# Rope columns of the second block's input projection as f32 column groups of the raw residual

## The chip, the core and the metric

The kernel runs on one core of a Trainium2 chip. The time is the device time of one execution in microseconds (us). Three runs of the kernel before gave 1178.18, 1178.46 and 1178.75 us; the median, 1178.46 us, is what the changed kernel is compared with. A core has five engines that run side by side and meet only at semaphores: PE (TensorE, the matrix engine), DVE (VectorE), ACT (ScalarE), POOL (GpSimd) and SP (SyncE, which here only issues transfers). Each engine takes its own instructions strictly in order.

## What is computed

Two transformer blocks over 512 tokens of 1024 features, all in f32. The change touches the start of the second block: a norm with a gain, a scale and a shift (the modulation), then one projection whose columns are the latent queries (256), the latent keys and values (128), the 32 rope columns of the keys, and the queries, keys and values of the chunked attention.

```python
h = modulate(rmsnorm_2(x, g_attn_norm[l]), sh_a, sc_a)      # h = norm * (1 + sc) + sh, per feature
proj = jnp.dot(h, w_in[l])
q_lat, kv_lat, k_rope, ca_qkv = jnp.split(proj, split_pts, axis=-1)   # 256, 128, 32, 1536 columns
...
k = jnp.concatenate([k_nope, broadcast(k_rope)], axis=-1)   # the same 32 columns for all 8 heads
k = rmsnorm_2(k, g_mla_k[l])
k = jnp.concatenate([k[..., :64], rope(k[..., 64:], positions)], axis=-1)
```

The input x of this block is itself a norm of the first block's result. Both norms divide by the root of a mean of squares over the features of one token, so together they are one factor per feature (`modA`) and one factor per token, called the root below; the shift `mod[:, 0, :]` is added behind both.

## The kernel before

**Layout and products.** Activations lie with the features on the 128 partitions and the 512 tokens along them, so a tile is 128x512. The residual is `h`, eight tiles (KD = 8). A product in f32 precision is made of three cheaper ones (`split_product`, L1550 is its matmul): each operand is split in a high and a low part of a reduced f32 type (`xh`, `xl` for activations, `wh`, `wl` for weights), and high·high, high·low and low·high are summed in PSUM. An output tile of 128 columns of the projection over 1024 features is so 8 x 3 = 24 matmuls. A matmul whose operands stay plain f32 needs no split; the trace shows it as two records.

**Weights.** They come in chunks of 128x2048, two slots each of `raw`, `wh` and `wl`. SP issues the transfer of chunk n once chunk n-2 has been split. ACT makes `wh` (`split_next`, `split_quarter`: L625, L643), once the products that read the slot before are done. POOL then makes `wl` = `raw` - `wh` (`low`, `low_edge`: L478, L506). PE waits for `lo_done`. So between "slot free" and "chunk usable" lie one ACT pass, one POOL pass and whatever stands ahead of them in these two queues.

**The place of the change.** In the second block's stream (`STREAM2`) the first chunk is "kvr": the latent keys and values (tile e=0) and the rope columns (tile e=1: the 32 columns twice and their halves swapped twice, 128 in all). The second, "ql", holds the two tiles of the latent queries, and four chunks "cqk" follow. `normed_pair` computes the two tiles of the first chunk in two halves of 256 tokens, while DVE (`norm_tiles`, L1104 and L1112) and ACT (`norm_high`, L683) still make `xh` and `xl` tile by tile: PE waits for each `norm.lo`. The root of a half stands in bank 2 or 3 (`SS_BANKS`, `rstd(j)`), the norm's tiles pass through banks 4, 5 and 7. Then PE computes the two ql tiles into banks 2 and 3, then the first cqk chunk into banks 6 and 7.

**ACT's order there** is written out by hand: the last `norm_high` tiles; `load_rel` (four transfers of the bias table, issued from ACT's own queue, L912 and L913); the logarithm and exponential of the final norm's sum (L662, L664); `split_next(base, ...)`, which is `wh` of the first cqk chunk (L625); the squares of the finished tiles (L931, L950). POOL's `wl` of that chunk (L478) comes behind the L625. DVE squares are split with L1430, the rope tile is turned by its cosines with L1436 to L1443.

**The same form elsewhere.** The first block has a projection of 8 columns padded to 32 that is done in plain f32 from the raw `h`: eight products 32 columns wide, each into its own quarter of the output partitions (L1826); a later product with a 0/1 matrix (`quarter_ones`, L1833) adds the four quarters. The changed kernel uses this form for the rope columns.

Of the kernel before, what the change touches and what calls it, by code (L numbers as in the profile page):

```python
# [7 lines left out]
ALU = mybir.AluOpType  # L8
# [41 lines left out]
STREAM2 = [("kvr", 1), ("ql", 1), ("cqk", PAIRS), ("cv", 2), ("mq", 1), ("mkv", 1), ("out", KD // 2), ("up", KF)]  # L50
# [37 lines left out]
def build(nc, x_first, xT, cols_in, stream1, down1, stream2, down2, ada, c_row, w_spatial_T, b_spatial_rows, w_gate, quarter_sum, positions, rel_tiles, outT):  # L88
    ctx = ExitStack()
    with ctx:  # L90
# [28 lines left out]
        sb("to_row", [P, ROW_PAD])  # L119
# [169 lines left out]
        rope.dve, rope.sq = sems("rope", "dve", "sq")  # L289
# [13 lines left out]
        P2 = {"kv": 1, "rope": 2, "ql": [3, 4], "q": [5, 7, 9, 11], "k": [6, 8, 10, 12], "v_first": 13, "v": [14, 15, 16, 17]}  # L303
# [68 lines left out]
        CSIL_HALVES = [ss_final, bank[7]]  # L372
        gate_raw, gate_weights = [lf[b][:, 0:KD * GATE_COLS] for b in range(2)]
# [101 lines left out]
        def _(pool):  # L475
# [83 lines left out]
            lows(N1, base - 1, DOWN_CHUNK)  # L559
            slot = (base - 1) % 2  # L560
# [58 lines left out]
        def _(act):  # L619
# [286 lines left out]
            act.dma_start(pos_i, positions.partition_broadcast(P)).then_inc(pos_landed, 16)  # L906
            residual_down(res_down1, norm_final, BASE1["down"], (cosines, sines))
# [7 lines left out]
            norm_rsqrt(norm_attn2, 0, eps2_c)  # L915

            def last_half():
# [3 lines left out]
                      | quarters(N1 + N_DOWN - 1, res_down1.mm, 2 * KD + 1, (9, 10, 11, 12)))  # L921
            act.wait_ge(res_down1.h, KD + 1)
# [21 lines left out]
            split_next(base, p2.mm, P2["rope"])  # L944
# [5 lines left out]
            act.activation(sqk[0][0:96, :], bank[1][0:96, :], ACT.Square).then_inc(rope.sq, 1)  # L950
            lat_square_high(0, sq2[0])
            head_square(sq2[1][:, :], bank[2][:, :], P2["ql"][0])
            act.wait_ge(norm_attn2.lo, 2 * KD)
            head_square(scratch[3][:, :], bank[3][:, :], P2["ql"][1])
            lat_square_high(1, sq2[1])
            lat_square_high(2, scratch[3])
            split_next(base + 1, p2.mm, P2["ql"][1])
            act.wait_ge(rope.sq, 1)
            act.activation(rope_sq[0:96, :], sqk[0][0:96, :], ACT.Copy).then_inc(rope.sq, 1)
# [111 lines left out]
        def _(dve):  # L1071
# [325 lines left out]
            def angles():  # L1397

                dve.wait_ge(pos_landed, 16)
# [52 lines left out]
            for t in range(2):  # L1452
                dve.scalar_tensor_tensor(scratch[2 + t][:, :], bank[2 + t][:, :], col("ql_g", t), r[:, :], ALU.mult, ALU.mult).then_inc(head.pre, 1)
# [93 lines left out]
        def _(pe):  # L1547
# [20 lines left out]
            def normed_pair(banks, slot, mm, norm, aside, at=3, quarter0=None):  # L1568


                for j in range(2):
                    for k in range(KD):
                        if j == 0 and k == at:
                            aside()
                        if quarter0 is not None and j == 0 and k in (0, 2, 4):
# [113 lines left out]
            def residual_down(L, res, base, norm):  # L1689
# [26 lines left out]
                for m, j, e in ((KD - 2, None, 0), (KD - 2, None, 1), (KD - 1, 0, 0), (KD - 1, 0, 1), (KD - 1, 1, 0), (KD - 1, 1, 1)):  # L1716
# [8 lines left out]
                    for kk in range(KF // 2):  # L1725
# [95 lines left out]
            pe.wait_ge(setup1, 10)  # L1821
            pe.wait_ge(p1.act, 1)
            for x in range(KD // QUARTERS):
                for quarter in range(QUARTERS):
                    k, c = QUARTERS * x + quarter, GATE_COLS * quarter
                    ins = pe.matmul(bank[4][c:c + GATE_COLS, :], gate_weights[:, GATE_COLS * k:GATE_COLS * k + GATE_COLS], h[:, k, :],  # L1826
                                    start=x == 0, stop=x == KD // QUARTERS - 1)
            ins.then_inc(p1.mm, 1)
# [85 lines left out]
            def last_sums():  # L1914
                norm_sum(norm_attn2, 1, weighted_acc, KD + 2)
# [3 lines left out]
            normed_pair(bank[0:2], base % 2, p2.mm, norm_attn2, last_sums, 5, KD + 6)  # L1919
            pe.wait_ge(lo_done, base + 2)  # L1920
            for e in range(2):
                features_tile(bank[2 + e], (base + 1) % 2, e).then_inc(p2.mm, 1)
            pe.wait_ge(setup2, 10)

            def pair_sums(p):
                for which in range(2):
                    if p == 0:
                        pe.wait_ge(lat.lo, 3)
# [293 lines left out]
```

## Time and profile before

| | us |
|---|---|
| median of 3 runs | 1178.46 |
| the profiled execution, its own time | 1179.01 |
| span of the profiled execution | 1177.3 |
| PE busy | 1167.2 (99%) |
| PE weight loads | 958.3 (81%) |
| DVE busy | 566.3 (48%) |
| ACT busy | 515.5 (44%) |
| POOL busy | 455.8 (39%) |

The span starts with the first recorded instruction; 1.7 us of the execution's own time lie around it. PE is busy almost all the time and its matmuls overlap in the records (a record of 0.39 us starts every 0.23 us), so for PE the distance between two starts is what a matmul costs, not its duration. Times of day in the text are microseconds from the start of the span of this execution. The granted clock of PE is 1.00 throughout.

### The profile page before, as it was taken

Reading aid. Unit: us, or ns where it says so; the run is one execution under the profiler, and the core shown is the slowest. Engines: PE = TensorE matmul, PEld = TensorE weight load, DVE = VectorE, ACT = ScalarE, POOL = GpSimd, SP = SyncE. Lnnn points to the kernel's source line nnn. Section 1 sums busy time; section 2 is a strip of 40 time slices with the busy share of each in tenths; the row PEclk is TensorE's granted clock in tenths of the full one; section 3 lists DMA queues with packets and bytes.
Section 4 is the critical chain, followed back from the end, with each engine's and each line's share of the span. In section 5 each row is a group of like instructions: output and inputs, shape, how many; then the busy total and the mean of one; then the engine's idle time right before and its main releaser. Section 6 shows DMA issues by size and latency. Waiting matters only on the chain.

```text
span 1177.3 us, 16124 instructions
## 1 busy us (share of the span) xinstructions
PE 1167.2 (99%) x5962; PEld 958.3 (81%) x5962; DVE 566.3 (48%) x1128; ACT 515.5 (44%) x815; POOL 455.8 (39%) x181
## 2 busy tenths in 40 slices
PE   9999999999999999999999999999999999999998
PEld 7787778988888888888988667789888888888887
DVE  4364245977777774212574567726434334440000
ACT  5534653634443432322646576835543443431110
POOL 6541314444434433444443211034434433434442
PEclk9999999999999999999999999999999999999999
DMA  8322122554554542223332110122232223212222
GB/s 302 115 82 98 36 103 78 215 188 174 209 204 171 196 156 94 92 95 110 141 134 77 55 37 1 37 72 74 106 108 102 76 107 107 79 66 99 99 98 96
DMA packets 27714, 132.06 MB, mean 112 GB/s; under 512 B 3472, under 2 KB 4880, under 8 KB 18832
## 3 DMA queue, kind: packets, MB, share of 16 engines
q1 hardware_dynamic: 25776, 128.90, 30.6%
q10 hardware_dynamic: 1888, 2.49, 0.7%
q8 instruction: 32, 0.52, 0.2%
q14 instruction: 18, 0.15, 0.0%
HBM read 129.28 MB, written 2.10 MB: 112 GB/s over the span
## 4 chain that ended last, share of the span: by engine, by line
PE 97%; ACT 2%; issue 0%; POOL 0%; DMA 0%; DVE 0%; DVEq 0%; ACTq 0%
PE psum L1550 86%; PE psum L1619 2%; PE psum L1631 2%; PE psum L2070 1%; PE psum L1780 1%; ACT prob L712 1%; PE psum L1883 1%; PE psum L2006 1%; ACT probT L695 1%; PE psum L1984 0%; POOL wl L494 0%; DMA gains_and_h<-x_first 0%; PE psum L1848 0%; PE psum L2014 0%; PE psum L1589 0%
## 5 line engine op out<-in xcount | busy, mean ns | idle before, releaser
L478 POOL TENSOR_TENSOR wl<-raw,wh 128x2048 fp32r<-128x2048 f32 (+1 forms) x88 | 364.6, 4143 | 497.5 <-ACT wh L628 285.0
L1550 PE MATMUL psum<-xh,wh 128*128 128x512 f32 (+1 forms) x1008 | 382.9, 380 | 1.2 <-POOL wl L494 1.1
L1550 PE MATMUL psum<-xl,wh 128*128 128x512 f32 (+1 forms) x1008 | 378.7, 376 | 0.0
L1550 PE MATMUL psum<-xh,wl 128*128 128x512 f32 (+1 forms) x1008 | 378.6, 376 | 0.0
L1196 DVE SCALAR_TENSOR_TENSOR scratch<-psum,cols,scratch 128x511 f32<-128x511 f32 (+1 forms) x176 | 131.6, 748 | 196.4 <-ACT scratch L773 188.4
L1550 PEld LDWEIGHTS psum<-xh,wh 128*128 128x128 f32 x1008 | 189.5, 188 | 40.1 <-issue 3.1
L1550 PEld LDWEIGHTS psum<-xh,wl 128*128 128x128 f32 x1008 | 189.6, 188 | 34.9
L1550 PEld LDWEIGHTS psum<-xl,wh 128*128 128x128 f32 x1008 | 189.7, 188 | 33.9 <-issue 0.2
L628 ACT ACTIVATE wh<-raw 128x2048 fp32r<-128x2048 f32 (+1 forms) x50 | 88.4, 1768 | 243.8 <-PE psum L1550 243.8
L1550 PE MATMUL psum<-acth,wh 128*128 128x512 f32 (+1 forms) x374 | 141.0, 377 | 0.0
L1550 PE MATMUL psum<-actl,wh 128*128 128x512 f32 (+1 forms) x374 | 140.8, 377 | 0.0
L1550 PE MATMUL psum<-acth,wl 128*128 128x512 f32 (+1 forms) x374 | 140.8, 377 | 0.0
L625 ACT ACTIVATE wh<-raw 128x2048 fp32r<-128x2048 f32 (+1 forms) x41 | 69.3, 1690 | 129.6 <-PE psum L1550 120.8
L1550 PEld LDWEIGHTS psum<-actl,wh 128*128 128x128 f32 x374 | 70.4, 188 | 13.0
L1550 PEld LDWEIGHTS psum<-acth,wh 128*128 128x128 f32 x374 | 70.4, 188 | 12.9
L1550 PEld LDWEIGHTS psum<-acth,wl 128*128 128x128 f32 x374 | 70.4, 188 | 12.8
L494 POOL TENSOR_TENSOR wl<-raw,wh 128x512 fp32r<-128x512 f32 (+1 forms) x28 | 35.5, 1298 | 112.7 <-ACT wh L643 99.8
L773 ACT ACTIVATE scratch<-psum,cols 128x512 f32<-128x512 f32 x88 | 67.6, 768 | 15.5 <-PE psum L1550 13.5
L1119 DVE SCALAR_TENSOR_TENSOR gains_and_h<-psum,mod,gains_and_h 128x512 f32 (+2 forms) x18 | 12.4, 690 | 125.1 <-PE psum L1550 125.1
L1080 DVE CUSTOM_DVE_ANT_0 ada_raw<-ada_raw,ss_final 128x512 f32<-128x512 f32 x42 | 55.2, 1315 | 0.0
L1117 DVE TENSOR_TENSOR gains_and_h<-gains_and_h,psum 128x512 f32<-128x512 f32 (+2 forms) x19 | 11.4, 599 | 80.0 <-PE psum L1550 80.0
L695 ACT ACTIVATE probT<-psum 128x256 f32<-128x256 f32 (+3 forms) x48 | 33.5, 697 | 34.1 <-PE psum L1619 34.1
(269 smaller groups left out, 1384.2 us busy)
## 6 DMA issues: line engine op xcount, KB each, us to landing
raw<-stream SPq DMA_DIRECT2D x69, 1024.0 KB, 4.8
ada_raw<-ada SPq DMA_DIRECT2D x48, 512.0 KB, 5.1
raw<-down SPq DMA_DIRECT2D x32, 704.0 KB, 4.0
outT<-gains_and_h SPq DMA_DIRECT2D x8, 256.0 KB, 5.0
gains_and_h<-xT SPq DMA_DIRECT2D x7, 256.0 KB, 6.4
raw<-stream SPq DMA_DIRECT2D x7, 256.0 KB, 6.8
rel<-rel_tiles ACTq DMA_DIRECT2D x1, 1344.0 KB, 8.7
wsT<-w_spatial_T SPq DMA_DIRECT2D x1, 512.0 KB, 6.1
```

What stands on the lines that cost most here:

```text
L478: pool.tensor_tensor(wl[slot][:, 0:w], raw[slot][:, 0:w], wh[slot][:, 0:w].bitcast(F32), ALU.subtract).then_inc(lo_done, 1)
L494: ins = pool.tensor_tensor(wl[slot][:, part], raw[slot][:, part], wh[slot][:, part].bitcast(F32), ALU.subtract)
L625: act.activation(wh[slot][:, 0:w], raw[slot][:, 0:w], ACT.Copy).then_inc(hi_done, 1)
L628: act.activation(wh[slot][:, 0:w], raw[slot][:, 0:w], ACT.Copy).then_inc(hi_done, 1)
L695: act.activation(probT[V % len(probT)][:, :, 0:w], TURN_BANKS[:, :, 0:w], ACT.Copy).then_inc(att.ptc, 1)
L773: act.activation(scratch[r][:, :], bank[r][:, :], ACT.Identity, bias=col(L.b, i * 4 + r), scale=col(L.w, i * 12 + (3 * r + 2))).then_inc(L ...
L1080: dve.tensor_tensor_reduce(part, part, c, 1.0, 0.0, ALU.mult, ALU.add, mod_sum[:, e, a:a + 1]).then_inc(ada_red, 1)
L1119: dve.scalar_tensor_tensor(h[:, m, tokens], b[:, tokens], mod[:, gain, bass.ds(m, 1)], h[:, m, tokens], ALU.mult, ALU.add).then_inc(res.h, 1)
L1196: dve.scalar_tensor_tensor(scratch[r][:, d:T], bank[r][:, 0:T - d], col(L.w, i * 12 + (3 * r + tap)), scratch[r][:, d:T], ALU.mult, ALU.ad ...
L1550: ins = pe.matmul(out, lhs[a], rhs[b], start=first and n == 0, stop=last and n == 2)
L1619: ins = pe.transpose(TURN_BANKS[:, e, P * j:P * j + P], prob[V % 4][:, e, P * j:P * j + P], ident[:, :])
L1631: ins = pe.matmul(HEADS_BANKS[p % 2][r:r + HD, P * i:P * i + P], v[:, j, c:c + HD], probT[V % len(probT)][:, e, P * j:P * j + P], start=j ...
```

## The change

The rope tile leaves the stream. Chunk one is now "kvq" (latent keys and values, and the first tile of the latent queries) and goes through `normed_pair`; chunk two holds the second query tile alone, half as wide (1024 columns). The rope columns are computed in plain f32 from the raw residual: POOL multiplies the 32 columns per feature tile by `modA`; PE makes eight products into four quarters of bank 4 (`rope_products`), inside the second half of `normed_pair`; ACT copies the quarters to SBUF; DVE multiplies them by the root; ACT adds the shift's share to them; PE adds up and spreads the quarters to the 128 rows with one f32 product with a 0/1 matrix (`rope_turned`), in the middle of the second query tile. The shift's share is eight one-column products of the unscaled columns with `mod[:, 0, k]`, put into the last residual tile of the first block, and copied by ACT behind the first root. The weights and the 0/1 matrix come with one more transfer from ACT's queue.

```diff
-STREAM2 = [("kvr", 1), ("ql", 1), ("cqk", PAIRS), ...
+STREAM2 = [("kvq", 1), ("ql", 1), ("cqk", PAIRS), ...
-    if n == BASE2["mkv"]:
+    if n in (BASE2["ql"], BASE2["mkv"]):
         return CHUNK // 2
...
+        rope_raw, rope_turned = scratch[0][:, 0:ROPE_COLS], scratch[0][:, ROPE_COLS:ROPE_COLS + P]
+        rope_weights = scratch[1][:, 0:ROPE_COLS]
+        rope_parts = bank[4]
+        rope_tile = bank[2]
+        SHIFTS = bank[3][:, 0:1]
+        ql_tiles = [bank[1], bank[3]]
...
             lows(N1, base - 1, DOWN_CHUNK)
+            pool.wait_ge(pos_landed, 32)
+            pool.wait_ge(mod_done, 7)
+            pool.tensor_tensor(rope_weights..., rope_raw..., modA[:, 0, :]..., ALU.mult).then_inc(mod_done, 1)
...
             act.dma_start(pos_i, positions.partition_broadcast(P)).then_inc(pos_landed, 16)
+            act.dma_start(scratch[0][:, 0:ROPE_COLS + P], w_rope[:, :]).then_inc(pos_landed, 16)
...
             norm_rsqrt(norm_attn2, 0, eps2_c)
+            act.wait_ge(p2.mm, P2["shift"])
+            act.activation(rope_shift[:, :], SHIFTS, ACT.Copy).then_inc(rope.act, 1)
...
             norm_high(norm_attn2, eps2_c, 0, ...)
+            act.wait_ge(p2.mm, P2["rope_parts"])
+            act.activation(scratch[2][:, :], rope_parts[:, :], ACT.Copy).then_inc(rope.act, 1)
+            act.wait_ge(rope.dve, 2)
+            act.wait_ge(rope.act, 1)
+            act.activation(scratch[2][:, :], scratch[2][:, :], ACT.Identity, bias=rope_shift[:, :]).then_inc(rope.act, 1)
             act.wait_ge(res_down1.h, KD + 1)
             load_rel(0, 0, 2)
             load_rel(1, 2, HEADS)
...
-            split_next(base, p2.mm, P2["rope"])
+            split_next(base, p2.mm, P2["ql"][0])
...
+            dve.wait_ge(rope.act, 2)
+            for j in range(2):
+                dve.tensor_tensor(scratch[2][:, half(j)], scratch[2][:, half(j)], rstd(j), ALU.mult).then_inc(rope.dve, 1)
...
-            for b, sq in enumerate((sq2[0], sq2[1], scratch[3])):
-                lat_square_low(b, sq)
+            lat_square_low(0, sq2[0])
+            lat_square_low(1, sq2[1])
...
             dve.tensor_copy(k_rope[0:64, :], k_rope[64:P, :]).then_inc(rope.dve, 1)
+            lat_square_low(2, scratch[3])
...
+            def quarter_products(out, columns, moving, ready, value):
+
+                pe.wait_ge(ready, value)
+                for x in range(KD // QUARTERS):
+                    for quarter in range(QUARTERS):
+                        k, c = QUARTERS * x + quarter, GATE_COLS * quarter
+                        ins = pe.matmul(out[c:c + GATE_COLS, :], columns[:, GATE_COLS * k:GATE_COLS * k + GATE_COLS], moving(k),
+                                        start=x == 0, stop=x == KD // QUARTERS - 1)
+                return ins
...
+                        if (j, e, kk) == (1, 0, 0):
+                            quarter_products(SHIFTS, rope_raw, lambda k: mod[:, 0, k:k + 1], mod_done, 8).then_inc(p2.mm, 1)
...
+            def rope_products():
+                pe.wait_ge(norm_attn2.lo, 2 * KD - 2)
+                quarter_products(rope_parts, rope_weights, lambda k: h[:, k, :], mod_done, 8).then_inc(p2.mm, 1)
+
-            normed_pair(bank[0:2], base % 2, p2.mm, norm_attn2, last_sums, 5, KD + 6)
+            normed_pair(bank[0:2], base % 2, p2.mm, norm_attn2, last_sums, 5, KD + 6, rope_products)
             pe.wait_ge(lo_done, base + 2)
-            for e in range(2):
-                features_tile(bank[2 + e], (base + 1) % 2, e).then_inc(p2.mm, 1)
+            pe.wait_ge(rope.dve, 2)
+            for k in range(KD):
+                if k == KD // 2:
+                    pe.wait_ge(rope.act, 3)
+                    pe.matmul(rope_tile[:, :], rope_turned, scratch[2][:, :], start=True, stop=True).then_inc(p2.mm, 1)
+                ins = split_product(ql_tiles[1][:, :], weights((base + 1) % 2, P * k, P * k + P), inputs(k), k == 0, k == KD - 1)
+            ins.then_inc(p2.mm, 1)
```

**ACT's queue at the start of the second block, before.** L683 is the last norm tiles, L912 and L913 the bias transfers, L662 and L664 the final norm, L625 `wh` of the first cqk chunk.

```order
L683 ACTIVATE xh<-psum,mod 128x256 [waits natt_tmp] x4
L912 DMA rel<-rel_tiles 128x2x448 [waits rd1_h]
L913 DMA rel<-rel_tiles 64x2x64
L912 DMA rel<-rel_tiles 128x6x448
L913 DMA rel<-rel_tiles 64x6x64
L662 ACTIVATE ss_acc<-psum,eps_c 128x512 [waits nfin_ss]
L664 ACTIVATE ss_acc<-ss_acc 128x512 [waits nfin_rstd]
L625 ACTIVATE wh<-raw 128x2048 [waits landed0,p2_mm]
L931 ACTIVATE sq<-psum 128x512 [waits p2_mm]
```

The same place now (L696 was L683, L926 and L927 were L912 and L913, L675 and L677 were L662 and L664, L638 was L625).

```order
L696 ACTIVATE xh<-psum,mod 128x256 [waits natt_tmp] x4
L939 ACTIVATE scratch<-psum 128x512 [waits p2_mm]
L942 ACTIVATE scratch<-scratch,rope_shift 128x512 [waits rope_act,rope_dve]
L926 DMA rel<-rel_tiles 128x2x448 [waits rd1_h]
L927 DMA rel<-rel_tiles 64x2x64
L926 DMA rel<-rel_tiles 128x6x448
L927 DMA rel<-rel_tiles 64x6x64
L675 ACTIVATE ss_acc<-psum,eps_c 128x512 [waits nfin_ss]
L677 ACTIVATE ss_acc<-ss_acc 128x512 [waits nfin_rstd]
L638 ACTIVATE wh<-raw 128x2048 [waits landed0,p2_mm]
```

The copy of the four quarters (L939) and the adding of the shift (L942), with their waits for PE and DVE, now stand ahead of the bias transfers, of the final norm and of `wh`.

**PE's queue between the first chunk and the second, now** (xh, xl: activations; wh0, wh1: high weights of the slots; scratch1: scaled rope weights). Rows that continue a product of three are left out where "..." stands.

```order
L1621 MATMUL psum<-gains_and_h,scratch1 32x512 [waits mod_done,natt_lo]
L1621 MATMUL psum<-gains_and_h,scratch1 32x512 x7
L1577 MATMUL psum<-xh,wh0 128x256 [waits natt_lo]
...
L1577 MATMUL psum<-xh,wh1 128x512 [waits rope_dve,lo_done]
...
L1965 MATMUL psum<-scratch2,scratch0 128x512 [waits rope_act]
...
L1577 MATMUL psum<-xh,wh0 128x512 [waits nfin_rstd,lo_done,setup2]
```

Before, the same place held the rest of the pair, 48 matmuls of the second chunk and then the first cqk chunk:

```order
L1550 MATMUL psum<-xh,wh0 128x256 [waits natt_lo]
L1550 MATMUL psum<-xl,wh0 128x256
...
L1550 MATMUL psum<-xh,wh1 128x512 [waits lo_done]
...
L1550 MATMUL psum<-xh,wh0 128x512 [waits nfin_rstd,lo_done,setup2]
```

The second chunk now holds 24 matmuls and the 0/1 product instead of 48 matmuls, and its first matmul waits for DVE as well.

## Rows read from the trace of the kernel before

**Rows 1.** The page, chain that ended last, shares of the span by engine.
```profile
PE 97%; ACT 2%; issue 0%; POOL 0%; DMA 0%; DVE 0%; DVEq 0%; ACTq 0%
```
**Rows 2.** Waits of PE: engine, line waited for, us in total, times, longest.
```profile
PE psum L1619 <- ACT probT L695: 2.8, 4, 1.3
PE psum L1550 <- POOL wl L494: 1.1, 1, 1.1
```
**Rows 3.** Timeline of PE, second half of the pair to the first cqk chunk: start, duration.
```profile
581.89 0.35 PE L1550 MATMUL psum<-xh,wh 128*128 128x256 f32 x1
...
583.38 0.40 PE L1550 MATMUL psum<-xh,wh 128*128 128x512 f32 x1
...
594.29 0.39 PE L1550 MATMUL psum<-xh,wh 128*128 128x512 f32 x1
```
**Rows 4.** Timeline of PE at the first block's four-quarter product.
```profile
52.18 1.92 PE L1826 MATMUL psum<-gains_and_h,lf 128*32 128x512 f32 x16
54.04 0.50 PE L1550 MATMUL psum<-wh,xh 128*128 128x512 f32 x1
54.38 0.40 PE L1550 MATMUL psum<-wl,xh 128*128 128x512 f32 x1
```
**Rows 5.** Timeline of DVE, the reader of that product.
```profile
54.17 0.69 DVE L1305 TENSOR_TENSOR lf<-psum,ss_final 128x512 f32<-128x512 f32 x1 [1.18 <-PE psum L1826]
```
**Rows 6.** Timeline of PE at a plain f32 product of 512 columns.
```profile
573.84 1.02 PE L1917 MATMUL psum<-ss_final,ones 128*128 128x512 f32 x2
574.30 0.68 PE L1550 MATMUL psum<-xh,wh 128*128 128x256 f32 x1
574.82 0.28 PE L1550 MATMUL psum<-xl,wh 128*128 128x256 f32 x1
```
**Rows 7.** Timeline of PE at eight plain f32 products of one column.
```profile
720.91 1.84 PE L2006 MATMUL psum<-ones,scratch 96*128 96x1 f32 x16
722.61 0.48 PE L1550 MATMUL psum<-wh,kvh 128*128 128x512 f32 x1
```
**Rows 8.** Timeline of PE's weight loads inside the four-quarter product.
```profile
52.18 0.16 PEld L1826 LDWEIGHTS psum<-gains_and_h,lf 128*32 128x32 f32 x8 [0.35 <-issue]
52.64 0.13 PEld L1826 LDWEIGHTS psum<-gains_and_h,lf 128*32 128x32 f32 x4 [0.30 <-issue]
```
**Rows 9.** Timeline of ACT and its transfer queue from the last norm tile on.
```profile
565.38 0.47 ACT L683 ACTIVATE xh<-psum,mod 128x256 fp32r<-128x256 f32 x1 [0.62 <-DVE psum L1104]
...
581.45 0.42 ACTq L912 DMA_DIRECT2D rel<-rel_tiles  x1
...
583.42 0.72 ACTq L913 DMA_DIRECT2D rel<-rel_tiles  x1
584.19 0.69 ACT L662 ACTIVATE ss_acc<-psum,eps_c 128x512 f32<-128x512 f32 x1 [2.27 <-issue]
...
585.44 1.90 ACT L625 ACTIVATE wh<-raw 128x2048 fp32r<-128x2048 f32 x1
```
**Rows 10.** Timeline of POOL in the same stretch.
```profile
554.68 3.38 POOL L566 TENSOR_TENSOR wl<-raw,wh 128x768 fp32r<-128x768 f32 x2 [3.73 <-ACT wh L762]
...
587.43 4.61 POOL L478 TENSOR_TENSOR wl<-raw,wh 128x2048 fp32r<-128x2048 f32 x1 [1.84 <-ACT wh L625]
...
598.07 4.60 POOL L478 TENSOR_TENSOR wl<-raw,wh 128x2048 fp32r<-128x2048 f32 x1 [6.04 <-ACT wh L625]
```
**Rows 11.** L1016, ACT's copies of a PSUM tile: duration min, median, max in ns.
```profile
L1016 ACT ACTIVATE v<-psum x4: 577/597/597, 719.3 to 724.3; 128x512 f32<-128x512 f32 x4
```
**Rows 12.** Timeline of DVE in the same stretch.
```profile
572.46 0.41 DVE L1088 TENSOR_TENSOR ss_final<-ss_final,psum 128x256 f32<-128x256 f32 x1
...
588.85 3.73 DVE L1430 TENSOR_TENSOR lat_low<-sq,lat_high 128x512 fp32r<-128x512 f32 x1 [6.42 <-ACT lat_high L947]
...
596.31 0.68 DVE L1430 TENSOR_TENSOR lat_low<-scratch,lat_high 128x512 fp32r<-128x512 f32 x1
...
599.21 4.01 DVE L1441 TENSOR_TENSOR rope_sq<-sqk,rope_sq 32x512 fp32r<-32x512 f32 x1
```
**Rows 13.** Timeline of PE, the first matmul of the final squares' sum in the next tile.
```profile
602.45 0.39 PE L1906 MATMUL psum<-lat_high,ones_all 128*128 128x512 f32 x1
```
**Rows 14.** Timeline of PE at the start of the span.
```profile
1.08 4.63 PE L1762 MATMUL psum<-ones 128*128 128x128 f32 x20 [1.08 <-POOL halfpi_c L513]
```

More of the change, by code:

```diff
@@ L49 @@
 STREAM1 = [("ua", 1), ("vg", 2), ("ub", 1), ("v", 2), ("qk", PAIRS), ("out", KD // 2), ("up", KF)]
-STREAM2 = [("kvr", 1), ("ql", 1), ("cqk", PAIRS), ("cv", 2), ("mq", 1), ("mkv", 1), ("out", KD // 2), ("up", KF)]
+STREAM2 = [("kvq", 1), ("ql", 1), ("cqk", PAIRS), ("cv", 2), ("mq", 1), ("mkv", 1), ("out", KD // 2), ("up", KF)]
 N1 = sum(n for _, n in STREAM1)
@@ L288, in build @@
         rope = Stage()
-        rope.dve, rope.sq = sems("rope", "dve", "sq")
+        rope.dve, rope.act = sems("rope", "dve", "act")
         head = Stage()
@@ L302, in build @@
               "q": [17, 19, 21, 23], "k": [18, 20, 22, 24]}
-        P2 = {"kv": 1, "rope": 2, "ql": [3, 4], "q": [5, 7, 9, 11], "k": [6, 8, 10, 12], "v_first": 13, "v": [14, 15, 16, 17]}
+        P2 = {"shift": 1, "rope_parts": 2, "kv": 3, "ql": [4, 6], "rope": 5, "q": [7, 9, 11, 13], "k": [8, 10, 12, 14],
+              "v_first": 15, "v": [16, 17, 18, 19]}
         MLA = {name: n + 1 for n, name in enumerate(
@@ L949, in _ @@
             head_square(sq2[0][:, :], bank[0][:, :], P2["kv"])
-            act.activation(sqk[0][0:96, :], bank[1][0:96, :], ACT.Square).then_inc(rope.sq, 1)
+            head_square(sq2[1][:, :], ql_tiles[0][:, :], P2["ql"][0])
             lat_square_high(0, sq2[0])
-            head_square(sq2[1][:, :], bank[2][:, :], P2["ql"][0])
+            lat_square_high(1, sq2[1])
+            act.wait_ge(p2.mm, P2["rope"])
+            act.activation(sqk[0][0:96, :], rope_tile[0:96, :], ACT.Square).then_inc(rope.act, 1)
+            act.wait_ge(rope.act, 4)
+            act.activation(rope_sq[0:96, :], sqk[0][0:96, :], ACT.Copy).then_inc(rope.act, 1)
             act.wait_ge(norm_attn2.lo, 2 * KD)
-            head_square(scratch[3][:, :], bank[3][:, :], P2["ql"][1])
-            lat_square_high(1, sq2[1])
+            head_square(scratch[3][:, :], ql_tiles[1][:, :], P2["ql"][1])
             lat_square_high(2, scratch[3])
             split_next(base + 1, p2.mm, P2["ql"][1])
-            act.wait_ge(rope.sq, 1)
-            act.activation(rope_sq[0:96, :], sqk[0][0:96, :], ACT.Copy).then_inc(rope.sq, 1)
             head_root(JOB_KV, P, bank[4])
@@ L1566, in features_tile, with normed_pair @@
                 return ins
-            def normed_pair(banks, slot, mm, norm, aside, at=3, quarter0=None):
+            def normed_pair(banks, slot, mm, norm, aside, at=3, quarter0=None, late=None):
                 for j in range(2):
@@ L1574, in normed_pair @@
                             aside()
+                        if j == 1 and k == KD - 2 and late is not None:
+                            late()
                         if quarter0 is not None and j == 0 and k in (0, 2, 4):
@@ L1820, in _ @@
                 features_tile(bank[6 + e], n % 2, e).then_inc(p1.mm, 1)
-            pe.wait_ge(setup1, 10)
             pe.wait_ge(p1.act, 1)
[L1823 to L1828, printed above, removed]
+            quarter_products(bank[4], gate_weights, lambda k: h[:, k, :], setup1, 10).then_inc(p1.mm, 1)
             def gate_sum():
@@ L1914, in last_sums @@
             def last_sums():
+                pe.wait_ge(rope.act, 1)
                 norm_sum(norm_attn2, 1, weighted_acc, KD + 2)
@@ L1928, in pair_sums @@
                         pe.wait_ge(lat.lo, 3)
+                        pe.wait_ge(rope.dve, 5)
                     else:
@@ L1944, in _ @@
                         pe.wait_ge(lat.lo, 3)
-                        pe.wait_ge(rope.dve, 3)
                     elif p == 3:
@@ L2142 @@
     w = f["w_in_2"][0]
-    x, xs = w[:, 384:416], np.concatenate([w[:, 400:416], w[:, 384:400]], 1)
-    kvr = np.concatenate([w[:, 256:384], x, x, xs, xs], 1)
+    turned = np.concatenate([np.arange(ROPE), np.arange(ROPE), (np.arange(2 * ROPE) + ROPE // 2) % ROPE])
+    w_rope = np.concatenate([w[:, 384:416].reshape(KD, P, ROPE).transpose(1, 0, 2).reshape(P, KD * ROPE),
+                             (np.arange(P)[:, None] % ROPE == turned[None, :]).astype(f32)], 1)
+    kvq = np.concatenate([w[:, 256:384], w[:, 0:P]], 1)
     ca = w[:, 416:]
```

29 lines of the change are left out of this document (17 added, 12 removed).

## The prediction

> **What bounds the kernel now.** I read the page's chain first: PE alone makes 97% of it [rows 1]. Then the list of PE's waits, to see whether anything else ever decides: its two longest entries are 2.8 and 1.1 us [rows 2]. So the kernel is a queue of matmuls without gaps. A matmul taken out is worth its distance to the next one, and any new wait of PE is paid in full. Then I read the timelines of PE, ACT, POOL and DVE around 580 us, where the change lands, to see by how much each weight chunk is early. That margin, and not PE's work, turns out to decide.
>
> **What leaves PE.** The rope tile is 24 matmuls. Between 583.38 and 594.29 PE starts 48 matmuls of 512 tokens, 0.227 us apart [rows 3]; the 24 that go are worth 5.45 us. They go from the second chunk, since the first query tile takes the rope tile's place in the first.
>
> **What PE gets.**
> 1. The eight products of the quarters. The first block does the same ones: from the group's start at 52.18 to the second matmul behind it at 54.38 are 2.20 us, less one ordinary distance of 0.23 makes 1.97 [rows 4], and with some 0.1 us ahead of the group (estimate) 2.05 us. Done one after the other, eight f32 products would cost 8 x 0.86 (item 2) = 6.9 us, so the row shows that the four quarters do run together.
> 2. The 0/1 product, one plain f32 product of 512 columns: from 573.84 to the second matmul behind it at 574.82 are 0.98 us, less one matmul of 256 tokens (0.12) = 0.86 us [rows 6].
> 3. The shift, eight one-column products into quarters. The trace has no such thing. Above stands the full-width form, 16 records in 1.70 us from 720.91 to 722.61, 1.8 with the slower restart [rows 7]; there each record waits for its weights. Below stands the pace of the weight loads in quarters, four in 0.13 us after a first group of eight in 0.16 [rows 8], with nothing for the columns: 0.3 us. I take 0.6: four rounds of 0.13 and the 0.1 of item 1. It is nearer to rows 8, since the shape is theirs. Both ends stay in the range.
> By the Trainium skill, "TensorEngine Tiling (Array Packing)", Instruction Overhead, each matmul costs about 60 cycles however few columns it has. By that alone the 16 records of the shift at the granted full clock would make 0.4 us, an estimate from that page and inside my bounds; the sum would end 0.2 us lower.
>
> PE's account so far is -5.45 + 2.05 + 0.86 + 0.6 = -1.9 us. If every wait were covered, the kernel would gain these 1.9 us, 0.16%.
>
> **What hides.** POOL's multiplication is 256 elements wide, an eighth of the 4.61 us of a 2048 one, 0.6 us, and POOL idles 3.73 us just behind its place [rows 10]. ACT's one-column copy behind the first root has an idle 0.62 us to fall into [rows 9]; without this cover it would delay the first norm tile by less than a 0.47 us ACT instruction. The second chunk's halves on ACT and POOL only come earlier. The extra transfer on ACT's queue stands a whole stage ahead.
>
> **PE's new wait for the root.** I work in the times of the trace before and add the shift at the end. The quarter products start behind the sixth feature tile of the second half, at 581.89 [rows 3], say 582.0. The first block's reader, DVE, starts 1.99 us behind the group's start [rows 4, 5], so the quarters can be read at 584.0. ACT's copy takes 0.60 [rows 11]: 584.6. DVE's two multiplications of 256 tokens take 0.41 each [rows 12]: 585.4. PE, having spent 2.05 us more than the 583.38 of before, finishes the pair at 585.43. So PE waits 0 to 0.3 us there; I take 0.1. Its second wait, for ACT's addition (0.6 us, 586.0), falls behind 12 matmuls (2.7 us) and costs nothing.
>
> **The term that decides: the next chunk's wh is queued behind that chain.** The order of ACT puts the copy and the addition, and with them the waits for PE and DVE, ahead of the four bias transfers, of the final norm and of L625. In the trace before the first transfer is issued at 581.45, and ACT is back at 584.19: 2.74 us of issuing, 2.27 of them shown as idle by "issue" [rows 9]. L625 starts 1.25 us later, at 585.44. POOL's L478 on it starts at 587.43, takes 4.61 and ends at 592.04 [rows 10]. PE needs the chunk at 594.29 [rows 3]. The margin is 2.25 us.
> After the change the first transfer can only be issued when the addition has started, at 585.4 instead of 581.45, 3.95 us later. Everything behind it keeps its distances: L662 at 588.2, L625 at 589.4, L478 from 591.4 to 596.0, PE at 596.1. PE itself, with the shorter second chunk, is ready at 585.5 + 5.45 + 0.86 = 591.8. It waits 4.3 us, more than all it had won: 596.1 - 594.29 = +1.8 us, and with the shift's 0.6 **+2.4 us**. No later chunk or tile gives this back, as PE is the bound again from there on.
>
> **The sum.** The profiled execution took 1179.01 us (span 1177.3 and 1.7 around it); with +2.4 it would be 1181.4. The median of the runs is 0.55 lower, 1178.46, so I predict **1180.9 us**. Own range of this case: +1.9 (shift 0.3, chain 0.2 shorter) to +3.9 (shift 1.8, chain 0.3 longer), 1180.4 to 1182.4. What a measurement can tell from no change is about 0.2%, 2.36 us; the forecast sits on that line.
>
> **Rivals.**
> A. *The chunk is not late (not slower).* Then PE's account stands: -1.8 with the 0.1 of the root wait, 1176.7 us. For it: PE never waits for L478 in the whole trace. Against: the order of ACT and a margin of 2.25 us against a delay of 3.95. It would need a chain shorter by 4.3 us. 0.08.
> B. *The delay is there, but the issuing isn't (not slower).* The 2.74 us of issuing could be a property of that moment before, for instance transfers of another queue in the way, and be gone 4 us later. Then the chunk comes 2.7 us earlier, PE waits 1.6 us, and the sum is 2.4 - 2.7 = -0.3: 1178.2 us. For it: only one such sequence is in the trace. Against: the first and the last of the four issues take 0.42 and 0.72 us, and the gap between them is filled [rows 9]. 0.10.
> C. *The clock falls in the new gap.* PE has no idle stretch over 1.3 us in this trace, so no row shows what 4.3 us do. Price: at the start, behind idle time, 20 records of 128 columns (10 products) take 4.63 us [rows 14]; at the pace of the 512-column product, 0.86 us, they would be a quarter of it each, 2.15 us. So falling back to the state of the start would cost 2.5 us more: 1183.4 us. The granted clock reads 1.00 even there, so the rows do not say that the start is the lower level; only the pace does. By the Trainium skill, "TensorE: Matmul & The Clock Gate", What's actually happening, the engine is held at half clock by default and an idle engine returns to it; the pace of rows 14 is in line with it, while the granted clock is not. 0.15.
> D. *The squares come late.* DVE's L1430 and L1441 took 3.73 and 4.01 us instead of 0.68 where POOL's L478 ran [rows 10, 12]: each ended just behind POOL's. Now the third L1430 stands behind L1441. With L478 on the next chunk at about 597.5 to 602.1, L1441 ends at 602.7, the small copy at 603.1 and the third L1430 at 603.8. PE wants it at 602.45 + 1.8 = 604.3 [rows 13] and 0.5 us later for its sum. If it misses, PE waits up to about 1 us: +3.0, 1181.5 us. 0.07.
>
> **Chances.** Forecast 0.60, A 0.08, B 0.10, C 0.15, D 0.07. Slower by over 0.2%: half of the forecast (0.31, what of its range lies above +2.36), C and D, together 0.53. Faster by over 0.2% needs A with the shift at its lower end and more: 0.04. Within 0.2%: the rest, 0.43. The range leaves out A and a part of B and C: 1178.9 to 1183.4.
>
> **What would show it.** In the profile after: PE idle about 4.3 us ahead of the first cqk chunk (583.4 + 8.9, about 592.4 with the shift), released by POOL's L478, now the largest entry of PE's waits; the first bias transfer about 4.5 us later than 581.45; L478 of that chunk ending near 596.6; the quarter products about 2 us and the 0/1 product 0.86; the shift group under 1 us; granted clock 1.00 behind the gap. The prediction is wrong if PE's idle time there is under 2 us, if the shift costs over 1.5 us, or if the matmuls behind the gap start more than 0.3 us apart.

## The result, and the profile after

The changed kernel takes 1184.23 us, median of 5 runs (1183.37 to 1184.64), against 1178.71 us of the kernel before in the same comparison (5 runs, 1178.18 to 1178.75). The ratio is 1.0047, with a 95% interval of 1.0037 to 1.0058: slower by 5.5 us. The forecast was 1180.9 us. The profiled execution took 1184.06 us, with a span of 1182.4 and a mean granted clock of 0.997. All 5 runs have 0.997 or 0.998. Of the 50 runs of the kernel before that the experiments below are compared with, 47 have 1.000 and three 0.999.

The page's chain still belongs to PE, with a share of "issue" that was 0% before [rows 1]:

```profile
PE 96%; ACT 2%; issue 1%; POOL 0%; DMA 0%; DVE 0%; DVEq 0%; ACTq 0%
```

The list of PE's waits (line waited for, us in total, times, longest) has one new entry at its top; the next is the longest of before [rows 2]. All numbers of the code moved: L1577 is L1550 of before, L487 is L478, L638 is L625.

```profile
PE psum L1577 <- issue: 4.7, 1, 4.7
PE psum L1658 <- ACT probT L708: 2.8, 4, 1.3
```

PE's timeline (start, duration; the answer to [rows 3]) has the quarters at 581.85, the 0/1 product at 588.18, and then the gap (a line that ends in x16 or x2 is several records in one):

```profile
581.85 1.92 PE L1621 MATMUL psum<-gains_and_h,scratch 128*32 128x512 f32 x16
583.71 0.39 PE L1577 MATMUL psum<-xh,wh 128*128 128x256 f32 x1
583.93 0.28 PE L1577 MATMUL psum<-xl,wh 128*128 128x256 f32 x1
...
588.18 1.02 PE L1965 MATMUL psum<-scratch 128*128 128x512 f32 x2
...
589.27 0.40 PE L1577 MATMUL psum<-xl,wh 128*128 128x512 f32 x1
...
591.58 0.39 PE L1577 MATMUL psum<-xh,wl 128*128 128x512 f32 x1
596.67 0.77 PE L1577 MATMUL psum<-xh,wh 128*128 128x512 f32 x1 [4.70 <-issue]
597.23 0.63 PE L1577 MATMUL psum<-xl,wh 128*128 128x512 f32 x1
597.66 0.63 PE L1577 MATMUL psum<-xh,wl 128*128 128x512 f32 x1
...
602.30 0.39 PE L1577 MATMUL psum<-xl,wh 128*128 128x512 f32 x1
```

Two things are to be seen. PE reaches the first cqk chunk at 596.67 instead of 594.29. And behind the gap the same matmuls stand 0.43 us apart until close to 602.30, and 0.23 from there on: the 13 distances from 596.67 to 602.30 take 5.63 us.

The table of stretches (us; busy time and count of PE, PEld, DVE, ACT, POOL; then PEclk) tells why: the engine stood idle through 592 to 596, and in the next stretch its clock was granted at 0.50, which is the 1.2 GHz level. The 0.93 of the idle stretch itself says that here the clock fell before PE started again. In the kernel before it was 1.00 in all of these stretches.

```profile
592.00:596.00 4.00, 0.00 (x0) 0.00 (x0) 2.51 (x1) 3.94 (x8) 3.95 (x1) 0.93 0.40 125
596.00:600.00 4.00, 3.33 (x8) 2.69 (x9) 3.87 (x6) 2.05 (x2) 2.44 (x2) 0.50 0.55 203
600.00:604.00 4.00, 4.00 (x14) 3.16 (x14) 3.94 (x3) 0.00 (x0) 2.69 (x1) 0.72 0.21 68
604.00:608.00 4.00, 4.00 (x19) 3.30 (x18) 0.42 (x1) 0.00 (x0) 0.00 (x0) 1.00 0.62 254
```

ACT and its transfer queue, the answer to [rows 9], show what PE waited for:

```profile
583.84 0.60 ACT L939 ACTIVATE scratch<-psum 128x512 f32<-128x512 f32 x1 [2.05 <-PE psum L1621]
585.26 0.72 ACT L942 ACTIVATE scratch<-scratch,rope_shift 128x512 f32<-128x512 f32 x1 [0.82 <-DVE scratch L1452]
585.26 0.40 ACTq L926 DMA_DIRECT2D rel<-rel_tiles  x1
585.70 0.70 ACTq L927 DMA_DIRECT2D rel<-rel_tiles  x1
586.43 0.60 ACTq L926 DMA_DIRECT2D rel<-rel_tiles  x1
587.07 1.69 ACTq L927 DMA_DIRECT2D rel<-rel_tiles  x1
588.81 0.69 ACT L675 ACTIVATE ss_acc<-psum,eps_c 128x512 f32<-128x512 f32 x1 [2.83 <-issue]
...
590.07 1.90 ACT L638 ACTIVATE wh<-raw 128x2048 fp32r<-128x2048 f32 x1
```

And POOL, the answer to [rows 10], ends the chunk's wl at 592.05 + 4.52 = 596.57, 0.1 us before PE starts:

```profile
592.05 4.52 POOL L487 TENSOR_TENSOR wl<-raw,wh 128x2048 fp32r<-128x2048 f32 x1 [8.36 <-ACT wh L638]
598.13 4.56 POOL L487 TENSOR_TENSOR wl<-raw,wh 128x2048 fp32r<-128x2048 f32 x1 [1.56 <-ACT wh L638]
```

The copy (L939) waits 2.05 us for the quarters, the addition (L942) 0.82 us for DVE, and the four transfers are issued behind both. PE lists its gap under "issue", not under POOL: the name there is what the profile could not assign, and POOL's end shows who released it.

One offset has to be taken out of the sum. Ahead of all that the change touches, the same POOL pass of 1408 elements stands 0.55 us earlier than before. In POOL's timeline of the kernel before:

```profile
547.74 3.21 POOL L478 TENSOR_TENSOR wl<-raw,wh 128x1408 fp32r<-128x1408 f32 x1 [4.25 <-ACT wh L625]
```

In that of the changed one:

```profile
547.19 3.22 POOL L487 TENSOR_TENSOR wl<-raw,wh 128x1408 fp32r<-128x1408 f32 x1 [4.25 <-ACT wh L638]
```

The offset arises within the first 10 us of the execution (another POOL pass starts at 9.18 before and at 8.40 now) and has stood at 0.55 since 142 us, so it isn't the change's. The late chunk costs 596.67 - 594.29 + 0.55 = 2.9 us, and the lower clock 2.6 us (13 distances in 5.63 us; in an experiment below, where the clock stays, the same 13 take 3.07). Together 5.5 us, which is the difference of the medians. The two profiled executions are 5.05 us apart, 5.6 with the offset.

### The profile page after: what moved, and what is told of

Same layout as the page of the kernel before. It is cut to its first block, busy times and chain, and to the rows that moved or that the text cites. A ratio compares the mean times of both kernels' runs of the same rounds, so it can differ in the third digit from the quotient of the medians.

```text
span 1182.4 us, 16156 instructions
## 1 busy us (share of the span) xinstructions
PE 1167.3 (99%) x5972; PEld 956.5 (81%) x5972; DVE 566.2 (48%) x1130; ACT 516.6 (44%) x818; POOL 454.4 (38%) x182
## 4 chain that ended last, share of the span: by engine, by line
PE 96%; ACT 2%; issue 1%; POOL 0%; DMA 0%; DVE 0%; DVEq 0%; ACTq 0%
PE psum L1577 86%; PE psum L1658 2%; PE psum L1670 2%; PE psum L2115 1%; PE psum L1821 1%; ACT prob L725 1%; PE psum L1918 1%; PE psum L2051 1%; ACT probT L708 1%; PE psum L2029 0%; POOL wl L503 0%; PE psum L1621 0%; DMA gains_and_h<-x_first 0%; PE psum L1883 0%; PE psum L2059 0%
## 5 line engine op out<-in xcount | busy, mean ns | idle before, releaser
L487 POOL TENSOR_TENSOR wl<-raw,wh 128x2048 fp32r<-128x2048 f32 (+1 forms) x88 | 364.5, 4143 | 504.3 <-ACT wh L641 284.8
L1577 PE MATMUL psum<-xh,wh 128*128 128x512 f32 (+1 forms) x1000 | 381.5, 382 | 5.9 <-issue 4.7
L1577 PE MATMUL psum<-xh,wl 128*128 128x512 f32 (+1 forms) x1000 | 376.5, 376 | 0.0
L1577 PE MATMUL psum<-xl,wh 128*128 128x512 f32 (+1 forms) x1000 | 376.5, 376 | 0.0
L1577 PEld LDWEIGHTS psum<-xh,wh 128*128 128x128 f32 x1000 | 188.8, 189 | 46.6 <-issue 9.3
L1577 PEld LDWEIGHTS psum<-xh,wl 128*128 128x128 f32 x1000 | 188.7, 189 | 34.7
L1577 PEld LDWEIGHTS psum<-xl,wh 128*128 128x128 f32 x1000 | 188.9, 189 | 33.7 <-issue 0.5
L1577 PE MATMUL psum<-acth,wh 128*128 128x512 f32 (+1 forms) x374 | 141.1, 377 | 0.0
L1577 PE MATMUL psum<-actl,wh 128*128 128x512 f32 (+1 forms) x374 | 140.8, 376 | 0.0
L1577 PE MATMUL psum<-acth,wl 128*128 128x512 f32 (+1 forms) x374 | 140.8, 376 | 0.0
L638 ACT ACTIVATE wh<-raw 128x2048 fp32r<-128x2048 f32 (+1 forms) x41 | 69.3, 1690 | 129.3 <-PE psum L1577 120.8
L1577 PEld LDWEIGHTS psum<-actl,wh 128*128 128x128 f32 x374 | 70.4, 188 | 13.0
L1577 PEld LDWEIGHTS psum<-acth,wl 128*128 128x128 f32 x374 | 70.4, 188 | 13.0
L1577 PEld LDWEIGHTS psum<-acth,wh 128*128 128x128 f32 x374 | 70.4, 188 | 12.7
```

Source lines behind the costliest of these rows:

```text
L487: pool.tensor_tensor(wl[slot][:, 0:w], raw[slot][:, 0:w], wh[slot][:, 0:w].bitcast(F32), ALU.subtract).then_inc(lo_done, 1)
L638: act.activation(wh[slot][:, 0:w], raw[slot][:, 0:w], ACT.Copy).then_inc(hi_done, 1)
L1577: ins = pe.matmul(out, lhs[a], rhs[b], start=first and n == 0, stop=last and n == 2)
```

## The experiments

My theory: the whole loss comes from the order of ACT, where the chunk's wh stands behind the chain of copy, addition and transfers, and its size is the late chunk plus the clock that falls in the gap. The rival: the new work on PE costs more than it looks (the quarters, the shift, the 0/1 product), or what slows the matmuls behind the gap is not the gap but the traffic of DVE and POOL beside them.

**The transfers behind the wh (changed kernel).** The chain of copy and addition stays.

```diff
                 act.activation(scratch[2][:, :], scratch[2][:, :], ACT.Identity, bias=rope_shift[:, :]).then_inc(rope.act, 1)
-            act.wait_ge(res_down1.h, KD + 1)
-            load_rel(0, 0, 2)
-            load_rel(1, 2, HEADS)
             act.wait_ge(norm_final.ss, 1)
...
             split_next(base, p2.mm, P2["ql"][0])
+            act.wait_ge(res_down1.h, KD + 1)
+            load_rel(0, 0, 2)
+            load_rel(1, 2, HEADS)
```

> The changed kernel with one edit: the four bias transfers stand behind the wh of the first cqk chunk in ACT's queue instead of ahead of it. Theory (the chunk is late, and the gap also lowers PE's clock): the wh starts about 3 us earlier, PE waits 1.5 to 2.5 us instead of 4.7 ahead of the first cqk chunk, the granted clock stays 1.00 behind it; 1178.8 us, 5.4 below the changed kernel. If the loss beyond the wait has nothing to do with the clock, only the 3 us of the wait go: 1181.3. Rival (the quarter products or the new waits on the root cost the time themselves): nothing changes, 1184.

Measured: 1178.72 us (11 runs) against 1178.50 (30 runs), ratio 1.0003 (0.9994 to 1.0012). With the issuing out of its way the wh starts at 587.21 instead of 590.07 (ACT's timeline):

```profile
587.21 1.90 ACT L638 ACTIVATE wh<-raw 128x2048 fp32r<-128x2048 f32 x1
```

PE's timeline has a gap of 1.8 us, and matmuls at full pace behind it:

```profile
593.88 0.47 PE L1577 MATMUL psum<-xh,wh 128*128 128x512 f32 x1 [1.79 <-issue]
594.18 0.39 PE L1577 MATMUL psum<-xl,wh 128*128 128x512 f32 x1
```

Moving four issues takes away all of the loss, 5.5 us, although they themselves take 3.6: the wh starts 2.9 us earlier, which is the late chunk, and the other 2.6 are the clock that no longer falls. All new work of PE is still there, and with a wait of 1.8 us on top the kernel takes no longer than the one before; so the new work is not dearer than what it replaces.

**The same move in the kernel before**, as a control: are the transfers themselves worth something anywhere?

```diff
-            act.wait_ge(res_down1.h, KD + 1)
-            load_rel(0, 0, 2)
-            load_rel(1, 2, HEADS)
             act.wait_ge(norm_final.ss, 1)
...
             split_next(base, p2.mm, P2["rope"])
+            act.wait_ge(res_down1.h, KD + 1)
+            load_rel(0, 0, 2)
+            load_rel(1, 2, HEADS)
```

> The kernel before with the bias transfers behind the wh of the first cqk chunk: the control for the order itself. Theory: the chunk was never late there, its margin grows from 2.25 to about 5 us, and nothing changes: 1178.7 us, within 0.3. Rival (the place of the transfers is worth something by itself): below 1178.

Measured: 1178.56 us (11 runs), ratio 1.0000 (0.9991 to 1.0009). No change: before, their place was covered by the margin of 2.25 us, and they cost only where the margin is spent. The margin grew less than expected, to 3.8 us: POOL's pass ends at 590.12 and PE needs it at 593.96, because the wh waits 0.42 us for the end of PE's pair (it starts at 583.25) and POOL starts its pass only at 585.51, behind its earlier work.

**The gap filled (changed kernel).** Five plain f32 products of 512 columns, whose result nobody reads, stand in the gap. The chunk stays as late as it is.

```diff
             ins.then_inc(p2.mm, 1)
+            for _ in range(5):
+                pe.matmul(bank[7][:, :], ones[:, :], ss_final[:, :], start=True, stop=True)
             pe.wait_ge(setup2, 10)
```

> The changed kernel with five plain f32 products of 512 columns (4.3 us, into a bank that the next product overwrites) put where PE waits for the first cqk chunk. They change nothing that is waited for. Theory: the wait is filled, PE's granted clock stays 1.00, the 12 matmuls behind it start 0.23 us apart instead of 0.43, and 2.7 us come back: 1181.6 us. Rival (the slow matmuls come from something else in that stretch, such as POOL and DVE at work beside them): still 0.43 apart, 1184.2.

Measured: 1181.60 us (8 runs), ratio to before 1.0027 (1.0017 to 1.0038): 2.6 us below the changed kernel, by doing more work (2.4 if each is taken against the runs of the kernel before beside it).

```profile
591.96 4.45 PE L1969 MATMUL psum<-ss_final,ones 128*128 128x512 f32 x10
596.79 0.47 PE L1577 MATMUL psum<-xh,wh 128*128 128x512 f32 x1 [0.38 <-issue]
597.10 0.40 PE L1577 MATMUL psum<-xl,wh 128*128 128x512 f32 x1
...
599.86 0.39 PE L1577 MATMUL psum<-xl,wh 128*128 128x512 f32 x1
```

From 596.79 to 599.86 are 13 distances in 3.07 us. DVE and POOL work beside them as in the changed kernel (L1467 takes 3.35 us here, 3.30 there), so their traffic is not what slowed the matmuls; the idle engine is. What is left, 1181.60 - 1178.50 = 3.1, is the late chunk alone (2.9 by the timelines above).

**The wh ahead of the addition (changed kernel).** If only the order of ACT is at fault, this should give what PE's account promised.

```diff
             act.activation(scratch[2][:, :], rope_parts[:, :], ACT.Copy).then_inc(rope.act, 1)
+            split_next(N1 + N_DOWN, p2.mm, P2["ql"][0])
             act.wait_ge(rope.dve, 2)
...
-            act.wait_ge(res_down1.h, KD + 1)
-            load_rel(0, 0, 2)
-            load_rel(1, 2, HEADS)
             act.wait_ge(norm_final.ss, 1)
...
-            split_next(base, p2.mm, P2["ql"][0])
+            act.wait_ge(res_down1.h, KD + 1)
+            load_rel(0, 0, 2)
+            load_rel(1, 2, HEADS)
```

> The changed kernel with ACT's queue in another order: copy of the quarters, wh of the first cqk chunk, addition of the shift, final norm, bias transfers. Theory: wh starts at about 585.3 us of the trace, POOL's pass on it ends near 592, PE is ready at 591.8 and waits 0 to 0.5 us; clock 1.00; PE's own account of the forecast (-1.9) remains: 1176.9 us, faster than the kernel before. The 0/1 product may wait up to 0.3 us for the addition, which is now 1.9 us later. Rival (the form itself is dearer than its matmul account): 1178.7 or above.

Measured: 1178.91 us (11 runs), ratio 1.0003 (0.9994 to 1.0012): missed by 2.0 us. PE starts the chunk at 592.38 with a wait of 0.17, as expected, but further on it now waits 1.5 us for DVE, until 602.75. PE, DVE and POOL of that place:

```profile
602.75 0.50 PE L1941 MATMUL psum<-lat_high,ones_all 128*128 128x512 f32 x1 [1.49 <-DVE lat_low L1456]
```

```profile
597.14 0.42 DVE L1469 COPY k_rope<-k_rope 64x512 f32<-64x512 f32 x1
597.59 5.11 DVE L1456 TENSOR_TENSOR lat_low<-scratch,lat_high 128x512 fp32r<-128x512 f32 x1
```

```profile
597.57 4.58 POOL L487 TENSOR_TENSOR wl<-raw,wh 128x2048 fp32r<-128x2048 f32 x1 [5.28 <-ACT wh L638]
```

The third difference of squares starts 0.02 us after POOL's pass and is held until that has ended. This is rival D, in a kernel where the gap no longer hides it.

**The third difference in front of the rope squares**, on top of the last kernel:

```diff
             dve.tensor_tensor(k_rope[64:P, :], rope_tile[64:P, :], turn[64:P, :], ALU.add).then_inc(rope.dve, 1)
+            lat_square_low(2, scratch[3])
             dve.wait_ge(rope.act, 5)
...
             dve.tensor_copy(k_rope[0:64, :], k_rope[64:P, :]).then_inc(rope.dve, 1)
-            lat_square_low(2, scratch[3])
```

> e2 (wh ahead of the addition, the transfers last) with DVE's third square difference moved from behind the key copy to ahead of the rope squares' difference (L1467). In e2 it started at 597.59, 0.02 us after POOL's second pass, took 5.11 us and made PE wait 1.5 us, 1.9 with the restart. Theory: it now starts near 596.4, ends before POOL's pass begins, PE's wait there is gone, and PE's own account remains: 1177.0 us, faster than the kernel before by 1.5. The rope squares' difference is the one that POOL now stretches, to about 602.7, which nothing waits for before 603. Rival: the 1.9 us come back in another wait (the key norm at 602.7 starts later and takes the next chunk with it): 1178.5 or above.

Measured: 1177.19 us (11 runs) against 1178.58 (20 runs), ratio 0.9988 (0.9979 to 0.9997). It has the whole change in it and is faster than the kernel before by 1.4 us, 0.12%. That is less than the 2.36 us that the prediction took for what a measurement can tell, but the two sets of runs don't overlap: the slowest of the 11 took 1177.72 us, the fastest of the 20 took 1178.27. DVE's and POOL's timelines show the third difference through at 596.79, 0.45 us before POOL starts. What POOL holds now is a copy that nobody waits for:

```profile
596.10 0.69 DVE L1456 TENSOR_TENSOR lat_low<-scratch,lat_high 128x512 fp32r<-128x512 f32 x1
596.82 0.69 DVE L1468 TENSOR_TENSOR rope_sq<-sqk,rope_sq 32x512 fp32r<-32x512 f32 x1
597.54 4.71 DVE L1470 COPY k_rope<-k_rope 64x512 f32<-64x512 f32 x1
```

```profile
597.24 4.72 POOL L487 TENSOR_TENSOR wl<-raw,wh 128x2048 fp32r<-128x2048 f32 x1 [5.29 <-ACT wh L638]
```

PE's account, -5.45 + 2.05 + 0.86 + 0.43 = -2.1 us, and 0.3 for two short waits (the root's and the chunk's 0.16) leave -1.8. The medians show -1.4; the other 0.4 us I can't place.

**A gap of chosen length in the kernel before.** Chained copies on ACT ahead of the transfers make the chunk late, with nothing else of the change. They tell whether a gap alone lowers the clock, and from what length.

```diff
+        idle = sem("idle")
...
+            for x in range(8):
+                act.wait_ge(idle, x)
+                act.activation(scratch[2][:, :], h[:, 0, :], ACT.Copy).then_inc(idle, 1)
             act.wait_ge(res_down1.h, KD + 1)
             load_rel(0, 0, 2)
```

With 8 copies:

> The kernel before, its rope columns as they were, with 8 copies of 512 columns (about 0.6 us each, one waiting for the other) put into ACT's queue ahead of the bias transfers. Theory: the first cqk chunk is late by about 4.8 us less its margin of 2.25; PE waits about 2.5 us; the clock may stay at 1.00, then 1181.0 us. If a delay of ACT alone did not cost PE this, the changed kernel's loss would have to come from its products: 1178.5.

With 10:

> The same with 10 copies: PE waits about 3.8 us. If the clock stays: 1182.3 us; if it falls as in the changed kernel (12 matmuls 0.43 us apart, 2.7 us): 1185.0.

With 12:

> The same with 12 copies: PE waits about 5.0 us, as long as in the changed kernel or longer. Theory: the granted clock falls to 0.50 behind the gap, 12 matmuls or so start 0.43 us apart: 1178.5 + 5.0 + 2.7 = 1186.2 us. Rival (the clock fell for something in the changed kernel alone): 1183.5.

Measured against 1178.58 us:

| copies | PE's wait in the profile | runs | median us | ratio (95%) | mean clock, executions |
|---|---|---|---|---|---|
| 8 | 2.37 | 9 | 1182.60 | 1.0030 (1.0020 to 1.0040) | 1.000 in 3, 0.998 in 6 |
| 10 | 3.67 | 4 | 1184.24 | 1.0045 (1.0030 to 1.0061) | 0.998 in 4 |
| 12 | 4.99 | 4 | 1185.69 | 1.0057 (1.0042 to 1.0073) | 0.997 or 0.998 in 4 |

PE behind the gap of 2.37 us, in an execution of the lower clock:

```profile
596.30 0.47 PE L1554 MATMUL psum<-xh,wh 128*128 128x512 f32 x1 [2.37 <-issue]
596.60 0.41 PE L1554 MATMUL psum<-xl,wh 128*128 128x512 f32 x1
596.84 0.60 PE L1554 MATMUL psum<-xh,wl 128*128 128x512 f32 x1
597.24 0.63 PE L1554 MATMUL psum<-xh,wh 128*128 128x512 f32 x1
...
600.22 0.42 PE L1554 MATMUL psum<-xl,wh 128*128 128x512 f32 x1
```

The first two matmuls still run at full pace and the clock falls only then, so the fall is not tied to the restart. With 10 copies it is the same: two distances at full pace, then eight slow ones. With 12 copies the clock is down at once, as in the changed kernel. The nine times of this kernel lie in two groups: 1181.07, 1181.22 and 1181.36 us at a mean clock of 1.000, and 1182.42 to 1183.21 us at 0.998. The first group is what the wait alone costs, 1178.58 + 2.6. The expectation of 1181.0 holds for this group only; the median is 1.6 above it. Of the runs with the wait of 1.8 us (transfers behind the wh) 10 of 11 had 0.999 or 1.000 and one had 0.998, at 1180.45 us, 1.7 above the median. Longer gaps lowered it in each of 8 executions, and the changed kernel's 4.7 us in each of 5. So a gap alone does it, and as far as these counts go the chance grows with its length. For the 10 copies the expectation with a falling clock was 1185.0, 0.8 too high: only eight distances are slow there, which is 1.6 us and not 2.7. For the 12 copies it was 1186.2, 0.5 too high; what the median lacks there stays open, the profiled execution took 1186.44.

## Why the prediction was too low

**The change's work on PE: right.** The quarters cost 583.93 - 581.85 = 2.08, less one distance of 0.12 and with the 0.09 ahead of them 2.05 us (predicted 2.05). The 0/1 product costs 589.27 - 588.18 - 0.23 = 0.86 (0.86). The shift, the only unseen operation, stands in this row of PE's timeline, between matmuls 0.12 apart:

```profile
560.80 0.28 PE L1577 MATMUL psum<-acth,wl 128*128 128x256 f32 x1
561.01 0.31 PE L1621 MATMUL psum<-mod,scratch 128*32 128x1 f32 x16
561.25 0.38 PE L1577 MATMUL psum<-acth,wh 128*128 128x256 f32 x1
561.47 0.28 PE L1577 MATMUL psum<-actl,wh 128*128 128x256 f32 x1
```

From 560.80 to 561.47 are 0.67 us instead of 0.24: 0.43 us (predicted 0.6, bounds 0.3 and 1.8). Rows of the same shape [rows 8] were the better bound than rows of the same column count [rows 7]. The estimate from the Trainium skill, "TensorEngine Tiling (Array Packing)", Instruction Overhead, was 0.4; the trace agrees for this shape, and not for the 16 full-width records of one column, which take 1.70 us [rows 7].

**The root's wait: right.** From the last matmul of the pair, 585.12, to the next, 585.37, are 0.25 us instead of 0.12: 0.1.

**The chunk queued behind the chain: right in place and mechanism, 0.5 us too early.** PE was to be ready at 592.4 and to start at 596.7 (596.1 and the shift); with the offset taken out it would be 592.4 and 597.2. What was late is the issuing. From the first issue to L675 are 588.81 - 585.26 = 3.55 us, not the 2.74 of [rows 9]: the fourth transfer's issue took 1.69 us instead of 0.72. The same 1.69 is in the kernel with the filled gap, where ACT does the same; 0.60 in the others of the changed kernel and in the three delayed ones, 0.88 in the control. What made it longer there stays open. The first issue was to come at 586.0 (585.4 and the shift) and came at 585.26 + 0.55 = 585.81; the missing 0.2 us are the shift's, so the chain of copy and addition was right. POOL's pass was 0.1 shorter. Together 0.8 - 0.2 - 0.1 = 0.5.

**The price of the gap: the step that failed.** The sum ended with "It waits 4.3 us, more than all it had won", and went on as if the engine came out of these 4.3 us as it went in. The fall of the clock stood among the rivals, as C, with 2.5 us and a chance of 0.15. It happened: the mean granted clock is down in each of the five runs, and in the profiled one it cost 2.6 us. The prediction's own sign of being wrong, matmuls more than 0.3 us apart behind the gap, showed with 0.43. The price came out right, but in part by luck: the pace was read from the slow start [rows 14], while nothing there says how long it lasts behind a gap. The ten products of the start happen to fill 4.6 us; behind the gaps of the runs the slow stretch had 8 to 12 matmuls and cost 1.6 to 2.6 us. The chance was too low. The start, where PE has been idle, is the only place in the trace where its pace is low, and that spoke for it; against it stood only the granted clock's 1.00 at that place, which the pace itself contradicts. A wait more than three times as long as any in the trace, with no row to show what it does, deserved a chance near the forecast's own. By the Trainium skill, "TensorE: Matmul & The Clock Gate", What's actually happening, the engine has two clock levels and idleness returns it to the lower; the 0.50 of the stretch behind the gap agrees. That a wait of 2.4 us did this in 6 of 9 executions and not in all is from the runs.

With the clock (2.6) and the chunk's start (0.5) the forecast's 1180.9 would have been 1184.0, within 0.3 us of the 1184.23 measured. The range ended at 1183.4 because it took C at its own middle value and gave it no spread, though C and the error of the chain can fall together. One chance was also counted wrong: of the forecast's own range, +1.9 to +3.9, three quarters lie above +2.36, not half, unless its middle weighs more than its ends.

**The rivals.** A (the chunk not late) and B (the issuing gone) are excluded by ACT's rows; the issuing was longer, not shorter. D (the squares held by POOL) did not cost anything in the changed kernel: L1467 took 3.30 us beside POOL, and the third difference came at 603.73, ahead of its reader. It cost 1.5 us of wait as soon as the chunk was on time.

## What to carry to other kernels

- Where a chunk or tile will be late, price the gap twice: the wait, and the slower matmuls behind it. Here a wait of 4.7 us cost 2.6 more, and one of 2.4 us cost 1 to 2 more in 6 of 9 executions. A gap of this length that can't be closed may be worth filling with matmuls nobody needs; here it gave back 2.6 us.
- On an engine that issues transfers and also prepares weights, put the weights first. An order that costs nothing while there is margin (the control) is all of the loss when a wait lands ahead of it.
- After closing a gap look for what it hid: the next late instruction was on DVE, and only moving that too turned the change into a gain.

## What the runs showed of the hardware

The granted clock can fall after PE has already run two matmuls again (8 copies, above), and it came back after 8 matmuls at 0.43 us (8 and 10 copies) or after 12 (12 copies, the changed kernel).

While POOL runs a pass, DVE instructions with a PSUM operand keep their time, and one that reads from SBUF and writes to SBUF, with no operand in PSUM, is held until POOL has ended. Both are in DVE's timeline of the changed kernel, beside POOL's pass from 598.13 to 602.69:

```profile
598.49 0.69 DVE L1463 TENSOR_TENSOR ada_raw<-psum,ada_raw 64x512 f32<-64x512 f32 x1
599.21 0.69 DVE L1465 TENSOR_TENSOR k_rope<-psum,ada_raw 64x512 f32<-64x512 f32 x1
599.94 3.30 DVE L1467 TENSOR_TENSOR rope_sq<-sqk,rope_sq 32x512 fp32r<-32x512 f32 x1
603.27 0.42 DVE L1469 COPY k_rope<-k_rope 64x512 f32<-64x512 f32 x1
```

I had not expected that a plain copy with one input is held as well: it takes 0.42 us here, behind POOL's pass, and 4.71 beside it in the fastest kernel. DVE instructions that only write SBUF are not held: beside POOL's pass from 472.94 to 476.16 in the kernel before, a MEMSET of 512 columns takes 0.48 us. So semaphores are not the only place where DVE and POOL meet. The Trainium skill, "GPSIMD Engine Reference", Key points, names as contending with POOL the DVE instructions with two SBUF inputs and those in a two-port mode. The rows agree for the first; for the copy they would agree if it runs in such a mode, which no row here shows.

The stages stand some 0.5 us apart from one execution to the next before the change has touched anything: the POOL pass of 547.74 and 547.19 above starts between 547.09 and 547.74 in the ten profiles of this case. A difference inside a stage is read only when this has been taken out.
